# Norm tiles in PSUM with a ScalarE copy, eight condition loads in each down stage, and four PSUM banks for its groups

## The reference

```python
x = x + jnp.square(jax.nn.relu(rms_norm(x, norm_mlp) @ w_up)) @ w_down        # first block, its last step

c_act = jax.nn.silu(c)
for l in range(2):
    mod = (c_act @ w_ada[l] + b_ada[l]).reshape(B, 9, 1024)
    h = modulate(rms_norm_2(x, norm_gain[l, 0]), mod[:, 0], mod[:, 1])
    x = x + 0.5 * mod[:, 2][:, None, :] * swiglu(h, ffn_w_gate[l, 0], ffn_w_up[l, 0], ffn_w_down[l, 0])
    h = modulate(rms_norm_2(x, norm_gain[l, 1]), mod[:, 3], mod[:, 4])
    x = x + mod[:, 5][:, None, :] * hybrid_mixer(h, w_in[l], ...)
    h = modulate(rms_norm_2(x, norm_gain[l, 2]), mod[:, 6], mod[:, 7])
    x = x + 0.5 * mod[:, 8][:, None, :] * swiglu(h, ffn_w_gate[l, 1], ffn_w_up[l, 1], ffn_w_down[l, 1])
```

## Time and profile before

| | |
|---|---|
| median of three runs | 3579.14 us (3577.69 to 3582.14) |
| the profiled execution's own time | 3572.99 us |
| its span | 3571.2 us |
| its mean granted TensorE clock | 0.979 |
| PE busy | 95% of the span |
| DVE, ACT, POOL busy | 50%, 39%, 57% |

### The profile page before, as it was taken

One profiled execution on the slowest core, in us unless ns is written; L12 is line 12 of the kernel. 1 busy time (PEld: TensorE's weight loads), 2 busy tenths in 40 slices (PEclk: granted clock), 3 DMA queues, 4 the chain that ended last, 5 costly groups with the idle time before them and its releaser, 6 DMA issues.

```text
span 3571.2 us, 52246 instructions
## 1 busy us (share of the span) xinstructions
PE 3382.1 (95%) x20538; PEld 2873.3 (80%) x20538; DVE 1788.9 (50%) x3466; ACT 1404.3 (39%) x2935; POOL 2039.0 (57%) x1242
## 2 busy tenths in 40 slices
PE   8878999888899999999999999999999999999999
PEld 6655777877788899866778989989997667789998
DVE  6554332656747666633123766576455332237444
ACT  2666551322234344255321523453442453215333
POOL 6514548355563675654667356646756546673665
PEclk9999999999999999999999999999999999999999
DMA  3222223255422652221233265224331222232332
GB/s 139 66 82 67 72 63 115 79 216 196 176 83 89 224 186 93 72 83 63 85 95 107 83 223 184 95 95 166 106 96 66 83 64 91 77 107 86 104 101 77
DMA packets 108276, 388.72 MB, mean 109 GB/s; under 512 B 12400, under 2 KB 12784, under 8 KB 98816
## 3 DMA queue, kind: packets, MB, share of 16 engines
q1 hardware_dynamic: 88272, 292.76, 24.7%
q10 hardware_dynamic: 19760, 92.62, 7.2%
HBM read 383.20 MB, written 2.13 MB: 108 GB/s over the span
## 4 chain that ended last, share of the span: by engine, by line
PE 78%; DVE 11%; DMA 4%; ACT 4%; issue 2%; ACTq 0%; POOL 0%; DVEq 0%; POOLq 0%
PE psum L1469 16%; PE psum L1471 15%; PE psum L1470 15%; PE psum L1538 8%; PE psum L1539 8%; PE psum L1540 8%; DMA ada_t<-ada_dram 4%; PE psum L1577 2%; DVE ada_t L2213 2%; PE psum L1619 2%; PE psum L1594 2%; PE psum L1563 1%; DVE rs_t L2079 1%; DVE h_lo L1996 1%; ACT a_hi L1952 1%
## 5 line engine op out<-in xcount | busy, mean ns | idle before, releaser
L1422 POOL TENSOR_TENSOR w_hi<-raw,ones 128x1024 fp32r<-128x1024 f32 (+2 forms) x405 | 685.2, 1692 | 605.8 <-PE psum L1471 598.1
L1437 POOL TENSOR_TENSOR w_hi<-raw,w_hi 128x512 fp32r<-128x512 f32 x376 | 481.5, 1295 | 795.7 <-ACT w_hi L1719 790.8
L1425 POOL TENSOR_TENSOR w_lo<-raw,w_hi 128x1024 fp32r<-128x1024 f32 (+2 forms) x405 | 863.4, 2132 | 31.8
L1469 PE MATMUL psum<-h_hi,w_hi 128*128 128x512 f32 (+1 forms) x1448 | 568.3, 392 | 34.1 <-DVE x L2374 14.7
L1471 PE MATMUL psum<-h_hi,w_lo 128*128 128x512 f32 (+1 forms) x1448 | 529.7, 366 | 0.0
L1470 PE MATMUL psum<-h_lo,w_hi 128*128 128x512 f32 (+1 forms) x1448 | 529.3, 366 | 0.0
L1538 PE MATMUL psum<-t_hi,w_hi 128*128 128x256 f32 x1504 | 435.1, 289 | 37.6 <-DVE t_lo L2021 27.1
L1469 PE MATMUL psum<-a_hi,w_hi 128*128 128x512 f32 (+1 forms) x1064 | 400.9, 377 | 45.5 <-DVE x L2374 40.0
L1539 PE MATMUL psum<-t_lo,w_hi 128*128 128x256 f32 x1504 | 431.8, 287 | 0.0
L1540 PE MATMUL psum<-t_hi,w_hi 128*128 128x256 f32 x1504 | 431.4, 287 | 0.0
L1470 PE MATMUL psum<-a_lo,w_hi 128*128 128x512 f32 (+1 forms) x1064 | 396.2, 372 | 0.0
(11 more groups left out here) (238 smaller groups left out, 6422.0 us busy)
## 6 DMA issues: line engine op xcount, KB each, us to landing
raw<-weights_dram SPq DMA_DIRECT2D x487, 512.0 KB, 3.6
ada_t<-ada_dram ACTq DMA_DIRECT2D x72, 1024.0 KB, 6.2
raw<-weights_dram SPq DMA_DIRECT2D x76, 256.0 KB, 2.6
raw<-weights_dram SPq DMA_DIRECT2D x32, 384.0 KB, 3.6
bias_t<-biases_dram ACTq DMA_DIRECT2D x36, 256.0 KB, 2.9
bias_t<-cum_dram ACTq DMA_DIRECT2D x16, 256.0 KB, 3.8
out_dram<-x SPq DMA_DIRECT2D x8, 256.0 KB, 2.0
raw<-weights_dram SPq DMA_DIRECT2D x4, 408.0 KB, 3.1
```

What stands on the lines that cost most here:

```text
L1422: nc.gpsimd.tensor_tensor(high, piece, ones[:, 0:1].to_broadcast([P, n]), ALU.mult)\
L1425: nc.gpsimd.tensor_tensor(w_lo[:, p % NR, 0:n], piece, high.bitcast(F32), ALU.subtract)\
L1437: nc.gpsimd.tensor_tensor(low_of(op), src, high_of(op).bitcast(F32), ALU.subtract)\
L1469: mm(dst, lh, rh, start=first, stop=False)
```

## The change

Three things change. First, quartered norms put their scaled tile into a PSUM bank (0 or 3) as the others do, and ACT copies it to `n_out` ahead of making `h_hi`; the sums of `quarter_sum` read `n_out` as before. ACT waits with that copy until the condition's sums are done, as `n_out` lies over `ada_t`. Second, every stage with a condition has 8 loads: three in `mlp` (24), and the first two of `ffn(0, 0)`, `ffn(0, 1)` and `ffn(1, 0)` (48). The loads are in the order of the layer's columns, and coefficients are made at other places: (0,0) after sum 12, (0,1) and (0,2) after sum 36, (1,0) after sum 48, (1,1) and (1,2) after sum 72. Third, down groups outside `close` take banks 6, 7, 4, 5 in turn. `UP_RING` is used by no group whose ring isn't set to other banks.

```diff
-ADA_FIRST, ADA_LATER = 3 * KC // ADA, 6 * KC // ADA
+ADA_FIRST, ADA_ALL = 3 * KC // ADA, 9 * KC // ADA
+ADA_PART = 8
...
-UP_RING, DOWN_RING = (2, 3, 0, 1), (4, 5)
+UP_RING, DOWN_RING, DOWN_FOUR = (0, 1, 2, 3), (4, 5), (6, 7, 4, 5)
...
 def norm_spread(m, half):
-    m.used, m.products = H_USED[0], TOTAL.get("product_done", 0)
+    m.used, m.products, m.ada = H_USED[0], TOTAL.get("product_done", 0), TOTAL.get("ada_used", 0)
...
 def norm_scale(m, c, half):
     n = tick("n_scaled")
     assert tick("h_hi") == n and tick("h_lo") == n
-    if m.quartered:
-        m.scales[c, half] = (n, None)
-    else:
-        b = m.nt[c % 2]
-        m.scales[c, half] = (n, take(b))
-        HELD[b] = ("h_lo", n)
+    b = m.nt[c % 2]
+    m.scales[c, half] = (n, take(b))
+    HELD[b] = ("h_lo", n)
...
-def down_groups(keys, n, src, res, norm=None):
+def down_groups(keys, n, src, res, norm=None, ring=DOWN_RING):
...
-        out.append(dense("down", keys[d], after, n=n, src=src, ring=DOWN_RING))
+        out.append(dense("down", keys[d], after, n=n, src=src, ring=ring))
...
-def with_ada(groups, n, stop):
+def with_ada(groups, stop):
...
-        out += [lambda: ada_sum(stop)] * sum(6 * k // n == i for k in range(n)) + [g]
+        out += [lambda: ada_sum(stop)] * sum(6 * k // ADA_PART == i for k in range(ADA_PART)) + [g]
...
-            jobs += with_ada(down_groups(keys, KC, "a", "one"), 10, 30)
+            jobs += with_ada(down_groups(keys, KC, "a", "one", ring=DOWN_FOUR), 3 * ADA_PART)
...
-    ada, stop = {(0, 0): ((9, 9, 0), 48), (0, 1): ((9, 9, 0), 66), (1, 0): ((6, 0, 0), 72), (1, 1): ((0, 0, 0), 0)}[l, n]
+    stop = ADA_PART * {(0, 0): 5, (0, 1): 7, (1, 0): 9, (1, 1): 0}[l, n]
...
-            groups = down_groups(keys, chunks, "a", (l, 2 * n))
-            jobs += with_ada(groups, ada[part], stop) if ada[part] else groups
+            groups = down_groups(keys, chunks, "a", (l, 2 * n), ring=DOWN_FOUR)
+            jobs += with_ada(groups, stop) if stop and part < 2 else groups
...
-            return n_out[:, c, columns(half)] if m.quartered else bank(m.nt[c % 2])[:, columns(half)]
+            return bank(m.nt[c % 2])[:, columns(half)]
...
                 E.wait_ge("product_done", m.products)
+                if m.quartered:
+                    E.wait_ge("ada_used", m.ada)
+                    fn(n_out[:, c, columns(half)], norm_tile(m, c, half), ACT.Copy).then_inc(sem["n_copied"], 1)
                 fn(h_hi[:, c, columns(half)], norm_tile(m, c, half), ACT.Identity,
```

More of the change, by code:

```diff
@@ L326 @@
     sums: int = 0
+    ada: int = 0
     @property
@@ L384, in norm_scale @@
         HELD[m.spread] = ("n_scaled", n)
+    if m.quartered:
+        tick("n_copied")
     put("nscale", m, c, half)
@@ L810, in ada_sum @@
         ada_load()
[L811 to L815, removed]
-def with_ada(groups, n, stop):
+    l, n = divmod(m + 1, ADA_ALL)
+    if n == ADA_FIRST:
+        put("coef", l, 0)
+    elif n == 0:
+        put("coef", l - 1, 1)
+        put("coef", l - 1, 2)
+def with_ada(groups, stop):
     def condition():
@@ L2207, in ada_sum @@
                 E.wait_ge(f"ada_loaded{m % 2}", 16 * (m // 2 + 1))
-                later = m - 2 * ADA_FIRST
-                l, c = (later // ADA_LATER, 3 * KC + ADA * (later % ADA_LATER)) if later >= 0 else \
-                    (m // ADA_FIRST, ADA * (m % ADA_FIRST))
+                l, c = m // ADA_ALL, ADA * (m % ADA_ALL)
                 for t in range(ADA):
@@ L2219, in coefs @@
                 c = 3 * n * KC
-                E.wait_ge("ada_used", 2 * ADA_FIRST + (n > 0) * (l + 1) * ADA_LATER)
+                E.wait_ge("ada_used", ADA_ALL * l + (ADA_ALL if n else ADA_FIRST))
                 v.tensor_tensor(mod[:, l, c:c + 3 * KC], mod_raw[:, l, c:c + 3 * KC],
@@ L2512 @@
     ada = w_ada_2.transpose(0, 2, 1).reshape(2, loads, ADA, P, D).transpose(0, 1, 3, 2, 4).reshape(2, loads, P, ADA * D)
-    ada = np.concatenate([ada[0, :ADA_FIRST], ada[1, :ADA_FIRST], ada[0, ADA_FIRST:], ada[1, ADA_FIRST:]])
+    ada = ada.reshape(2 * loads, P, ADA * D)
     i, j = np.arange(P)[:, None], np.arange(P)[None, :]
```

## The result

The changed kernel takes 3518.81 us, the median of four runs (3510.53 to 3520.58), beside 3578.94 us for the kernel before (3577.69 to 3582.14). The ratio is 0.9826, with a 95% interval of 0.9809 to 0.9843. The gain is 60.1 us; 64.5 us had been forecast, as 3514 us. Later, in a group of runs of its own, the same kernel read 3511.94 us and the kernel before 3578.42 us, a gain of 66.5 us. The profiled execution of the changed kernel took 3520.51 us, its span is 3518.7 us, and its granted clock 0.984 (before: 3571.2 us and 0.979).

A forecast was written before the change was run, and what follows sets the result against it. PE, 95% busy, was taken as the bound, let down by waits for DVE's x additions; 49.5 us (banks and sums) + 15 us (norm) = 64.5 us, from 3579.1 to 3514 us, range 3494 to 3540 us.

The forecast's parts named there:

- The waits: Down groups of stages with condition sums: all 40.0 us of PE's waits for x additions go.
- I charge 2 us for the first stage and 2 us for all others: Ends of stages with condition sums: next set's first products wait for late x additions, 4 us charged, bounds 0 to 18.
- they have the same room: First two stages of `ffn(1, 0)`: the two more and eight new sums have the same room as in `ffn(0, 0)`.
- Group d now waits for x addition d - 4: Down groups with four banks: each x addition has 10.9 us more time, so 40.0 us of PE's waits go.
- The clock: Clock drops behind PE's waits go: 13.5 us in down stages, 8 us at quartered norms.
- The first part: Four banks and eight sums a stage: 40.0 + 13.5 - 4 = 49.5 us gain, bounds 22 and 53.5 us.
- The second part: Quartered norms' tile in PSUM: 7 us of waits and 8 us of clock, 15 us gain, bounds -4 and 22.5.
- I take 1.0 us left of each wait of 2.4: Five quartered norms: PE's wait for an x addition falls by 1.4 us each, 7 us in all.
- Rival 2: Stage ends: PE's wait moves there, 3 to 4 us in each of nine stages; gain 15 to 35 us; chance 0.11.
- Rival 1: Quartered norms: not faster, as ACT's queue keeps x additions late; 3528 to 3534 us; chance 0.10.
- Rivals 3 and 4: Slower, stage-end waits exceeding all gains, 3590 us, chance 0.03; no effect, PE waiting for `a_lo` or POOL, 3579 us, 0.02.
- I am wrong if product matmuls (line 1538) wait for x additions or DVE's `w_hi` for more than 10 us in all: Sign against the forecast: product matmuls wait over 10 us in all for x additions or DVE's `w_hi`.

## Why the prediction was right, and where not

**The waits.** Forecast: 40.0 us out of the down groups, some of it back. Measured: none is left in the groups, as predicted. The waits for x additions fell from 54.6 to 2.7 + 13.2 = 15.9 us.

**Waits at the stages' ends.** This is the term that was mis-sized: 4 us were charged and 13.2 us appeared (5.4 us in the second profile). The step "I charge 2 us for the first stage and 2 us for all others" failed twice. In the first stage the estimate put the x addition of group 6 at 764.9 and it ended at 763.2. The wait of 1.77 us for the forecast 2.0 is partly luck, as PE was 1.4 us sooner at the end of the stage too (761.5 for 762.9). And I stopped there. Bank 5 needs the x addition of group 7 as well, with four weight instructions ahead of it, and that costs a second wait of 1.64 us. And "they have the same room" was wrong for the first stage of `ffn(1, 0)`: it gave 4.9 us alone, the largest, where its loads' median landing was 7.3 us. I had taken 6.2 us throughout. In the second profile this stage gave 0.4 us.

**What does the work.** The prediction wrote the 40.0 us to four banks: "Group d now waits for x addition d - 4", with 10.9 us more time. As a statement on the groups that is right, but for the time it is the wrong half. Four banks alone gain 13 us and only move the waits; loads and coefficient places alone gain 25 us; both 43 us. Since the change has both parts, the sum did not suffer. The prediction's own arithmetic had it: ten sums need as much as the whole stage. The tail of ten sums was never priced apart. Nor was the time of the coefficient steps, 8.0 us for two of them in the kernel before: the prediction only said that 10.9 us of new room cover them. They took 10.5 us in `ffn(0, 0)` of the changed kernel, and no wait stands behind them, so that held, with 0.4 us to spare.

**The clock.** Forecast: 13.5 + 8 = 21.5 us. The sum of lost clock fell from 75.0 to 54.7 us, 20.3 us. In the profiles these waits and the clock give 38.7 + 20.3 = 59.0 us, against 52.5 us of span; some 3.5 us of it stand in other entries of the waits (POOL's `w_lo` 2.3 us more, `s_sb` 0.8, `w_hi` 0.4), and 3 us I can't place.

**The first part.** Forecast 49.5 us, measured alone 43.1 us. Its profile has 9.8 us of waits at the sets' starts, 5.8 us more than charged; this is about the difference of 6.4 us, though the interval of the run is 5 us to each side.

**The second part.** Forecast 15 us, bounds -4 and 22.5. Measured 17 to 19 us alone, and 21 us as the cost of undoing its one operand. The mis-sized step is "I take 1.0 us left of each wait of 2.4": no wait for an x addition was left, and all 11.9 us of them went. The 2.3 us for POOL's `w_lo` at the norm of `ffn(1, 0)` are new, so 9.6 us went in all, 9.1 us of them at the other four norms, where 7 us had been forecast for all five. The row that it leant on, the mixer's norm, still waits 1.33 us; its half groups are shorter, which I had named and then not used. The copies took 385 ns (388 forecast), `h_lo` 481 ns (near 480), and the scaling into PSUM 486 ns. Of the 65 ns that the rule on DVE's overhead in PSUM would charge (the Trainium skill, Perfetto Trace Analysis, "Optimizing Scalar/DVE Operations"), these durations show 13 ns for the scaling (486 against 473) and nothing for `h_lo`: from PSUM it takes 481 ns in the mean, and from SBUF before, the median of its 64 was 480 ns too; only those beside POOL raised the mean to 728.

**The two errors** have opposite signs: 6 us too much for the first part, 2 to 6 us too little for the second. That the total came within 4.4 us of the forecast is in part luck, as these errors cancel.

**The rivals.** Rival 2, the wait at the end of the stage, named the right mechanism. It came at less than half of its price (3 to 4 us in each of nine stages): 13.2 us in five stages, and the clock mostly didn't fall behind waits of 1 to 2 us. Landings rose by 0.6 us, not 1. Rival 1 is refuted by the norm's runs. Rivals 3 and 4 had no support in any run. The sign "I am wrong if product matmuls (line 1538) wait for x additions or DVE's `w_hi` for more than 10 us in all" came true by its letter in both profiles (13.2 + 10.9 and 5.4 + 11.8 us), while the time stayed in the forecast's range. It could tell nothing: the waits for DVE's `w_hi` alone were 10.5 us in the kernel before.

## What to carry to other kernels

More buffers between a producer and a consumer move a wait to where the run ends; they remove it only if the producer has caught up by then. Add up what stands in the slower engine's queue up to the last item of the stage, compare it with the stage's length, and spread the work until the last one is in time. Take the durations from the trace, those of the smallest instructions too: here eight of them took 8 us. Then look which buffers the next stage asks for first, and let those be the ones whose last use comes first: here one line, worth 9.5 us by the medians. Where a VectorE instruction with both inputs in SBUF stands beside a busy GpSimd ahead of work that others wait for, it can pay to give it one input from PSUM, even at the price of a copy on ScalarE: here 17 to 21 us.

## What the runs showed of the hardware

The landing time of the 1 MB loads isn't a constant of the kernel: the medians are 6.1 to 6.8 us over eleven profiles of kernels that move the same bytes, and the changed kernel read 6.8 us in one profile and 6.4 us in the other. Its waits went with it, 13.2 and 5.4 us, and its runs lie from 3507 to 3522 us. A load of half the size took 4.6 us, in a kernel that is otherwise the one whose whole loads took 6.8 us. I had not expected that a single operand's place could be worth 21 us in 3500. And a VectorE instruction on 128x8 numbers took 2.2 us beside GpSimd's splits of the weights, where it takes 0.17 us without them.
